# Token-shift layer: pair scores inside receptance and gate tiles, banks of both engines, the below-diagonal work shared anew

## What is computed

```python
def rwkv7_time_mix(h, mu, w_r, w_k, w_v, w_o, w0, w1, w2, a0, a1, a2, g1, g2, k_k, k_a, r_k, ln_g, ln_b):
    xx = jnp.pad(h, ((0, 0), (1, 0), (0, 0)))[:, :-1] - h
    xr, xw, xk, xv, xa, xg = [h + xx * mu[i] for i in range(6)]
    r = xr @ w_r
    w = -jax.nn.softplus(-(w0 + jnp.tanh(xw @ w1) @ w2)) - 0.5
    k = xk @ w_k
    v = xv @ w_v
    a = jax.nn.sigmoid(a0 + (xa @ a1) @ a2)
    g = jax.nn.sigmoid(xg @ g1) @ g2
    ...
    def step(state, inp):
        r_t, d_t, k_t, v_t, kk_t, a_t = inp
        sa = jnp.einsum('bhij,bhj->bhi', state, -kk_t)
        state = (state * d_t[:, :, None, :] + sa[..., None] * (kk_t * a_t)[:, :, None, :]
                 + v_t[..., None] * k_t[:, :, None, :])
        return state, jnp.einsum('bhij,bhj->bhi', state, r_t)
```

## Time and profile before

| what | us |
|---|---|
| median of three runs | 1712.45 |
| profiled execution, device time | 1714.71 |
| its span, first to last instruction | 1712.9 |
| PE busy (share of the span) | 1660.0 (97%) |
| DVE busy | 1031.1 (60%) |
| ACT busy | 397.2 (23%) |
| POOL busy | 274.6 (16%) |

### The profile page before, as it was taken

One profiled execution on the slowest core, in us unless ns is written; L12 is line 12 of the kernel. 1 busy time (PEld: TensorE's weight loads), 2 busy tenths in 40 slices (PEclk: granted clock), 3 DMA queues, 4 the chain that ended last, 5 costly groups with the idle time before them and its releaser, 6 DMA issues.

```text
span 1712.9 us, 26789 instructions
## 1 busy us (share of the span) xinstructions
PE 1660.0 (97%) x11020; PEld 1314.6 (77%) x11020; DVE 1031.1 (60%) x1990; ACT 397.2 (23%) x1033; POOL 274.6 (16%) x356
## 2 busy tenths in 40 slices
PE   8999999999999999999999899999999999998998
PEld 7997488776699946999467779699946777676774
DVE  5777344754287664876578766487673554625563
ACT  2010023532210102011036532311002233222331
POOL 3324000000023200323001323122200220012100
PEclk9999999998999999999999999999999999999999
DMA  8767654221445453645444320345456973469830
GB/s 267 224 190 228 145 132 147 74 74 52 145 153 192 149 196 124 196 149 195 149 117 148 122 98 2 98 148 184 161 181 118 167 109 94 99 93 182 118 104 24
DMA packets 197113, 237.68 MB, mean 139 GB/s; under 512 B 28349, under 2 KB 177265, under 8 KB 196737
## 3 DMA queue, kind: packets, MB, share of 16 engines
q1 hardware_dynamic: 192016, 225.36, 47.2%
q0 software_dynamic: 4960, 10.61, 2.2%
q10 hardware_dynamic: 16, 0.00, 0.0%
HBM read 232.69 MB, written 1.07 MB: 136 GB/s over the span
## 4 chain that ended last, share of the span: by engine, by line
PE 88%; DVE 5%; ACT 2%; DMA 2%; issue 1%; POOL 0%; SPq 0%; DVEq 0%; POOLq 0%; ACTq 0%
PE ps L605 29%; PE ps L277 23%; PE ps L671 14%; PE ps L522 6%; PE ps L615 3%; DMA arena<-arena 2%; PE ps L1939 2%; PE ps L2578 1%; PE ps L2590 1%; PE ps L1956 1%; PE ps L2609 1%; PE ps L335 1%; PE ps L2604 1%; PE ps L1719 1%; DMA ring<-in_ffn_w_gate 0%
## 5 line engine op out<-in xcount | busy, mean ns | idle before, releaser
L277 PE MATMUL ps<-hT,ring 128*128 128x272 f32 (+3 forms) x1664 | 353.2, 368 | 1.8 <-ACT hT L359 1.3
L277 PEld LDWEIGHTS ps<-hT,ring 128*128 128x128 f32 x1664 | 286.3, 193 | 51.1 <-issue 6.8
L605 PE MATMUL ps<-arena,ring 128*128 128x128 f32 x1280 | 162.5, 275 | 0.0
L671 PE MATMUL ps<-ring,arena 128*128 128x512 f32 x352 | 155.9, 593 | 1.7 <-DVE more L776 1.7
L866 POOL TENSOR_TENSOR arena<-arena 128x128 f32<-128x128 f32 x44 | 36.7, 834 | 740.3 <-DVE arena L790 396.6
L605 PEld LDWEIGHTS ps<-arena,ring 128*128 128x128 f32 x1280 | 152.6, 192 | 0.0
L605 PE MATMUL ps<-hT,ring 128*128 128x128 f32 x1280 | 150.1, 275 | 0.0
L605 PEld LDWEIGHTS ps<-hT,ring 128*128 128x128 f32 x1280 | 146.5, 192 | 0.0
L671 PEld LDWEIGHTS ps<-ring,arena 128*128 128x128 f32 x352 | 66.6, 190 | 87.2 <-issue 87.2
L605 PE MATMUL ps<-arena 128*128 128x128 f32 x960 | 120.3, 275 | 0.0
L605 PEld LDWEIGHTS ps<-arena 128*128 128x128 f32 x960 | 113.6, 192 | 0.0
(11 more groups left out here) (490 smaller groups left out, 2693.9 us busy)
## 6 DMA issues: line engine op xcount, KB each, us to landing
ring<-in_ffn_w_gate SPq DMA_DIRECT2D x44, 1024.0 KB, 5.4
ring<-in_ffn_w_up SPq DMA_DIRECT2D x44, 1024.0 KB, 7.2
ring<-in_ffn_w_down SPq DMA_DIRECT2D x44, 1024.0 KB, 5.0
ring<-in_w_in SPq DMA_DIRECT2D x32, 1024.0 KB, 14.2
ring<-in_ab_w_in SPq DMA_DIRECT2D x12, 1024.0 KB, 5.2
ring<-in_w_out SPq DMA_DIRECT2D x8, 1024.0 KB, 5.0
ring<-in_ab_w_out SPq DMA_DIRECT2D x6, 1024.0 KB, 4.8
ring<-in_c_w_k SPq DMA_DIRECT2D x4, 1024.0 KB, 6.3
```

Source lines behind the costliest of these rows:

```text
L277: last = nc.tensor.matmul(o, l, r, start=(i == 0), stop=(i == len(pairs) - 1))
L605: m = nc.tensor.matmul(o, left[:, k, :], right[:, k, :], start=(k == 0), stop=(k == 3))
L671: return nc.tensor.matmul(ps[:, BANK[i], :], hid[p][:, left, :], right, start=(p == 0), stop=(p == LAST))
```

## The change

The scores of pairs 0, 1 and 2 are now computed inside r4 (after 3 of its 8 products), r5 (after 7) and r7 (after 3), and those of pair 3 inside the gate's first layer. Each pair takes its first bank from ScalarE's ring and its second from VectorE's, before the tile around it takes its own. ScalarE still empties every bank below the diagonal (of VectorE's ring too, where it raises `dve_out`) and copies the diagonals of the first banks and of (0, 1). VectorE copies the diagonals of (1, 1), (2, 1) and (3, 1), and leaves L2281 and L2282 to ScalarE. The bonus product and the first gate pair go ahead of the 32-row rounds; the rounds of chunk 1 (`m32`, `t32` with t = 1) go to ScalarE's banks and copies.

```diff
             def r_product(j):
-                tile_product("r", j, S_R + j // 2, MB[3], (2 if j == 0 else 1) if j % 2 == 0 else 0)
+            def r_product(j, p2=None, at_c=0):
+                slot = S_R + j // 2
+                if j % 2 == 0:
+                    take_slot(pe, slot)
+                o = score_banks(p2) if p2 is not None else None
+                n = turn_a("r", j)
+                for c in range(KD):
+                    if o and c == at_c:
+                        pair_scores(p2, o)
+                    m = nc.tensor.matmul(bank_a(n)[:, 0:S], slot8(slot)[:, c, (j % 2) * P:(j % 2 + 1) * P], MB[3][:, c, :],
+                                         start=(c == 0), stop=(c == KD - 1))
...
-            pair_scores(0)
-            r_product(4)
-            pair_scores(1)
-            r_product(5)
-            pair_scores(2)
+            r_product(4, 0, 3)
+            r_product(5, 1, 7)
             r_product(6)
-            pair_scores(3)
-            r_product(7)
+            r_product(7, 2, 3)
...
+            last = score_banks(3)
             n = turn_a("g1")
             group(bank_a(n)[:, 0:S], [(g1[:, c, 0:P], MB[5][:, c, :]) for c in range(KD)], 1)
+            pair_scores(3, last)
...
+            def bank_32(t, name):
+                return bank_d(turn_d(name, t)) if t == 0 else bank_a(turn_a(name, t))
...
+            take_slot(pe, s)
+            pe.wait_ge(act_out, job["g1",])
+            bonus_product()
+            gate_pair(0)
+            pe.wait_ge(act_out, job["x", 3, 0])
+            pe.wait_ge(dve_out, job["x", 3, 1])
             pe.wait_ge(sc_dve, 1)
             m32_product(0)
-            take_slot(pe, s)
-            pe.wait_ge(act_out, job["g1",])
-            gate_first(0, 0)
             m32_product(1)
-            gate_first(0, 1)
-            gate_first(1, 0)
+            gate_pair(1)
             pe.wait_ge(sc_dve, 2)
             t32_product(0)
-            gate_first(1, 1)
-            bonus_product()
             pe.wait_ge(sc_act, 1)
             t32_product(1)
-            for r, (t, h) in enumerate((t, h) for t in range(T) for h in range(2)):
...
@@ rwkv_act
+            def below_out(p2, hh):
+                _, left, corner = score_parts(score_bank(p2, hh), p2, hh)
+                nc.scalar.activation(*left, ACT.Copy)
+                nc.scalar.activation(*corner, ACT.Copy).then_inc(dve_out if hh else act_out, 1)
+
             def scores_out(p2):
...
+                act_a()
+                diagonal_out(p2, 0)
+                below_out(p2, 0)
...
             key_root(7)
+            decays(6)
+            diagonal_out(0, 1)
+            decays(7)
             scores_out(1)
-            decays(6)
             r_out(5)
-            decays(7)
-            scores_out(2)
             r_out(6)
-            scores_out(3)
+            act_a()
+            diagonal_out(2, 0)
+            diagonal_out(3, 0).then_inc(x_out, 1)
+            below_out(2, 0)
             r_out(7)
+            act_a()
+            below_out(3, 0)
+            below_out(0, 1)
+            act.wait_ge(x_out, 2)
+            for p2 in (1, 2, 3):
+                below_out(p2, 1)
...
+            gate_out(0)
+            b = next_a().rearrange("p (h n) -> p h n", h=SH)
+            nc.scalar.activation(m32[32:64, SH:2 * SH, :], b[32:64], ACT.Copy)
+            nc.scalar.activation(m32[96:P, SH:2 * SH, :], b[96:P], ACT.Copy).then_inc(act_out, 1)
+            gate_out(1)
+            b = next_a().rearrange("p (h n) -> p h n", h=SH)
+            nc.scalar.activation(tts[1][0:32, :, 32:64], b[0:32], ACT.Copy)
+            nc.scalar.activation(t64[32:64, SH:2 * SH, 0:32], b[32:64], ACT.Copy)
+            nc.scalar.activation(tts[1][64:96, :, 96:P], b[64:96], ACT.Copy).then_inc(act_out, 1)
...
@@ rwkv_dve
-            diag, left, corner = score_parts(next_d(), 3, 1)
-            for o, b in diag:
-                m = nc.vector.tensor_copy(o, b)
+            dve_d()
+            for p2 in (1, 2, 3):
+                for o, b in score_parts(next_d(), p2, 1)[0]:
+                    m = nc.vector.tensor_copy(o, b)
             m.then_inc(x_out, 1)
...
-            nc.vector.tensor_copy(*left)
-            nc.vector.tensor_copy(*corner).then_inc(dve_out, 1)
```

More of the change, by code:

```diff
@@ L1708, in pair_scores @@
                             if t == 1 and i == 1:
-                                m.then_inc(to_dve if p2 == 3 and hh == 1 else to_act, 1)
+                                m.then_inc(to_dve if hh else to_act, 1)
             need_h(pe, pe_h.n)
@@ L1837, in t64_product @@
                                         start=True, stop=True, skip_group_check=True)
+            def bank_32(t, name):
+                return bank_d(turn_d(name, t)) if t == 0 else bank_a(turn_a(name, t))
             def m32_product(t):
-                n = turn_d("m32", t)
+                b = bank_32(t, "m32")
                 for h in range(SH):
@@ L1843, in m32_product @@
                     for g in range(2):
-                        m = nc.tensor.matmul(bank_d(n)[64 * g + 32:64 * g + 64, 32 * h:32 * h + 32],
+                        m = nc.tensor.matmul(b[64 * g + 32:64 * g + 64, 32 * h:32 * h + 32],
                                              at0[:, ch, :] if g == 0 else at64[64:96, ch, 32:64], t64[64 * g:64 * g + 32, ch, 0:32],
                                              start=True, stop=True, skip_group_check=True)
-                        if ch == 0 and g == 0:
-                            m.then_inc(slot_used, 1)
-                m.then_inc(to_dve, 1)
+                m.then_inc(to_act if t else to_dve, 1)
             def t32_product(t):
-                pe.wait_ge(dve_out, job["m32", t])
-                n = turn_d("t32", t)
+                pe.wait_ge(act_out if t else dve_out, job["m32", t])
+                b = bank_32(t, "t32")
                 for h in range(SH):
@@ L1857, in t32_product, with gate_pair @@
                         lo, hi = slice(64 * g, 64 * g + 32), slice(64 * g + 32, 64 * g + 64)
-                        nc.tensor.matmul(bank_d(n)[lo, 32 * h:32 * h + 32], m32[hi, ch, :], tts[t][hi, h, hi],
-                                         start=True, stop=True, skip_group_check=True)
[L1860 to L1866, removed]
+                        m = nc.tensor.matmul(b[lo, 32 * h:32 * h + 32], m32[hi, ch, :], tts[t][hi, h, hi],
+                                             start=True, stop=True, skip_group_check=True)
+                        if ch == 0 and g == 0:
+                            m.then_inc(slot_used, 1)
+                    m = nc.tensor.matmul(b[32:64, 32 * h:32 * h + 32], tts[t][32:64, h, 32:64], m32[32:64, ch, :],
+                                         start=True, stop=True, skip_group_check=True)
+                m.then_inc(to_act if t else to_dve, 1)
+            def gate_pair(t):
+                for h in range(2):
+                    m = nc.tensor.matmul(bank_a(turn_a("g2", t, h)), sg1[:, t * P:(t + 1) * P], slot2(s)[:, 0, h * 512:(h + 1) * 512],
+                                         start=True, stop=False)
+                    if t == 0 and h == 0:
+                        m.then_inc(slot_used, 1)
+                for h in range(2):
+                    r = 2 * t + h
+                    rows = slice(32 * r, 32 * r + 32)
+                    nc.tensor.matmul(bank_a(job["g2", t, h]), sg2[rows, :], slot2(s)[rows, 1, h * 512:(h + 1) * 512],
+                                     start=False, stop=True).then_inc(to_act, 1)
             def bonus_product():
@@ L2010, in next_a, with score_bank, diagonal_out @@
                 return bank_a(n)
-            def scores_out(p2):
-                for hh in range(1 if p2 == 3 else 2):
-                    diag, left, corner = score_parts(next_a(), p2, hh)
-                    for o, b in diag:
[L2016 to L2020, removed]
+            def score_bank(p2, hh):
+                n = job["x", p2, hh]
+                act.wait_ge(to_dve if hh else to_act, n)
+                return (bank_d if hh else bank_a)(n)
+            def diagonal_out(p2, hh):
+                for o, b in score_parts(score_bank(p2, hh), p2, hh)[0]:
+                    m = nc.scalar.activation(o, b, ACT.Copy)
+                return m
+            def below_out(p2, hh):
+                _, left, corner = score_parts(score_bank(p2, hh), p2, hh)
+                nc.scalar.activation(*left, ACT.Copy)
+                nc.scalar.activation(*corner, ACT.Copy).then_inc(dve_out if hh else act_out, 1)
+            def scores_out(p2):
+                act_a()
+                diagonal_out(p2, 0)
+                below_out(p2, 0)
             def key_root(j):
@@ L2110, in rwkv_act, with gate_out @@
                 m.then_inc(act_out, 1)
-            for t in range(T):
+            def gate_out(t):
                 for h in range(2):
```

42 lines of the change are left out of this document (17 added, 25 removed).

## The result

| | before | changed |
|---|---|---|
| median of 20 runs, us | 1713.93 | 1720.68 |
| lowest and highest, us | 1709.68, 1721.96 | 1713.28, 1726.1 |
| profiled execution and its span, us | 1714.7, 1712.9 | 1713.28, 1711.5 |

The account below looks back on a forecast made before the run. TensorE, with 88% of the chain, was taken as the bound. Value products 3.0 us ahead, -1.5 for the clock, +0.6 - 0.45 later gave 1.6 faster: 1710.9 us from 1712.45, range 1705.5 to 1715.5.

Parts of the forecast that it names:

- The failed step: From m64 on: nothing edited, weight loads' slot releases all come earlier or within 1 us, so no cost.
- the sum: Whole change: value products 3.0 ahead, clock's fall -1.5, later part +0.6 - 0.45, giving 1.6 us faster.
- the walk: Step-by-step timing of the engines through the token-shift stage; finds TensorE's wait moved to receptance tile 7, 4.1 us.
- The clock's fall: Behind the 4.1 us wait before receptance tile 7: granted clock falls to half, costing 1.5 us.
- rival D: VectorE's later solve ends last, delaying the first t32 or m32 round; 0.4 to about 2 us slower; chance 0.15.
- ScalarE's list: From 943.8, copies, roots and decays without gap sum to 10.7 us; pair 1's first bank comes free at 954.6.
- The value products: Behind the gate's first layer: first one starts at 966.2 against 969.1, 3.0 us ahead, 1.5 with the clock's fall.
- The solve: On VectorE: transpose at 965.6 against 962.99, then near 967, four later; t32 rounds keep 0.6 us of slack.
- The copies on ScalarE: Second 32-row rounds: 32x512 copy taken as 0.59 us against VectorE's 0.68; TensorE waits 0.3 to 0.5 us at m64.
- The wait on L2113: Between gate seconds and token rows: TensorE's 0.6 us wait for this gate copy goes.
- Within 0.5%: Whole kernel's time: chance 0.92 of staying within about 0.5% (8.6 us), 0.05 for faster, 0.03 for slower.
- The range: Whole kernel's time: 1705.5 to 1715.5 us, around a forecast of 1710.9.

Follow-up runs that it names:

- Run 1: Changed kernel with the gate weights' slot release put back to the first token transpose; median 1718.71 us, ratio to before 1.0014.
- run 5: Changed kernel with late slot release, pair 1's first bank emptied early, and gate pair 1 split ahead of and between t32 rounds; median 1711.78 us, ratio 0.9992.
- run 6: Each half of the change alone: new scores with the tail of before, ratio 1.0118; scores of before with the new tail, ratio 1.0052.
- run 2: Changed kernel with ScalarE emptying pair 1's first bank right after key root 7; median 1712.45 us, ratio to before 0.9980.
- run 7: New scores with the tail of before, plus ScalarE emptying pair 1's first bank right after key root 7; median 1711.29 us, ratio to before 0.9980.
- run 4: Kernel before with an extra 1 MB copy within HBM, started by the first t32 product; ratio to before 1.0012.
- run 3: Changed kernel with both the slot release put back and pair 1's first bank emptied early; median 1711.40 us, ratio to before 0.9987.
- the front alone: Kernel before with only the new scores, banks and shared diagonals, tail from the first 32-row round unchanged; median 1738.62 us, ratio 1.0118.

## Why the prediction was wrong

- **The failed step** is one clause of the sum: "From m64 on nothing is edited, and the weight loads wait for slots six loads ahead whose releases all come earlier or within 1 us." I used it to price the moved release at nothing. As a fact it holds: the gate slot's release comes 2.9 us earlier from r3's end (68.0 for 70.9). What fails is that an earlier load costs nothing. What matters is not when the load can start, but what TensorE is doing while it runs. The load lands on a dense train of small instructions and on the fetch of those behind it, and TensorE stands 2.4 to 3.3 us in the next group. Run 1 shows the release alone (2.76 to 1.12), run 5 the train (1.35 to none). Price of the step, by the chunk product's start from r3's end: 5.9 later where the forecast had it 1.6 earlier.
- **What the change does to TensorE's order** I costed only through its waits. Gate and bonus products moved from between the t32 rounds and behind them to places ahead of them, and I counted their time; that they had also parted the trains of small products was not in the walk.
- **The clock's fall** was in the sum once, behind r7, and near its price (1.8 measured, 1.5 forecast). A second one, at the stop, lengthened the busy time by 3.9 us and was in no case. In rival D I had the size of such a thing ("a clock fall of twice the length"), with the wrong cause.
- **ScalarE's list was right**: 10.7 us from 943.8 forecast, 10.9 measured from the start of S0's first bank (940.86) to the end of L2045; r7 waits 3.80 for 4.1. On ScalarE:

```profile
946.79 1.56 ACT L2039 ACTIVATE arena<-ps 32x128 f32<-32x128 f32 x4
...
949.71 1.55 ACT L2039 ACTIVATE arena<-ps 32x128 f32<-32x128 f32 x4
951.27 0.38 ACT L2044 ACTIVATE hT<-ps 128x256 f32<-128x256 f32 x1
951.55 0.25 ACT L2045 ACTIVATE more<-ps 32x128 f32<-32x128 f32 x1
```

- **The value products**, 1.4 ahead forecast with the clock's fall, 0.6 measured: r7 starts 0.2 later from r3's end than in the walk (17.5 for 17.3), the half clock took 0.3 more, and the first value product waits 0.56 for 0.3.
- **The solve** starts 4.9 us later from r3's end than before (30.5 for the earlier trace rows's 25.6), forecast 4. In the changed kernel nobody waits for it: VectorE is ready at 1000.8 for the t32 rounds, TensorE comes at 1002.4. Rival D did not happen. In the order of run 6, with nothing ahead of the rounds, the same late solve costs 2.20 us.
- **The copies on ScalarE**: 32 x 512 took 0.59 us against VectorE's 0.68, as taken from the 128 x 512 copy.

```profile
1004.72 0.59 ACT L2167 ACTIVATE arena<-ps 32x512 f32<-32x512 f32 x1 [1.09 <-PE ps L1876]
```

- **The wait on L2113** (0.6) did go, and m64 did not wait for these copies. That is the stop's doing: in run 5, which has none, m64 waits 0.71 us for them, where the forecast had 0.3 to 0.5.
- **Slips in the walk**: the list of the idling before leaves out 0.36 us before the third score group, r6 is 8.0 us ahead by the walk's own figures and not 7.7, and the value products 2.9 and not 3.0. Only the last is in the sum.
- **The chances.** "Within 0.5%" held. The range did not: it was made of waits on semaphores alone, and its upper end had no case in which a stop of no known releaser and a ten-microsecond clock fall come together.

## What to carry to other kernels

A slot release is the start time of a transfer. When an edit moves one, look at what the engines run in the 3 to 5 us after it, and keep the load off dense trains of small matmuls; put a few long products between such trains instead of ahead of them. Where two engines share the emptying of banks, walk the list of the slower one in its written order and put the bank that TensorE needs first at its head: that one reordering (run 2) turned 0.34% slower into 0.2% faster, with the interval below 1, and run 7 reached the same. These two are the versions to take; run 5 has the shortest stretch, but its median does not show it.

## What the runs showed of the hardware that I had not expected

**TensorE can run out of instructions.** The stops of 1.1 to 3.3 us have no releaser, full DMA engines lengthen them, and spacing the train removes the one of 1.35. This is the reading that fits all eight profiles with the new tail, seven with a stop and the spaced one without. The packets of q8 in the kept traces bear it out: at each of these seven stops, and at that of run 4, TensorE goes on 1.3 to 1.6 us behind a packet's end, though the stops range from 0.89 to 3.31 us. With no load under way (runs 1 and 3) that packet starts 1.5 to 1.6 us behind the first t32 product; with the load that this product releases, 2.8 to 3.5. The Trainium skill, "Runtime: NRT & Kernel Launch", section "Instruction fetch mechanics", says that the sequencer fetches the next page by a DMA queue of its own while it runs the current one, and that the cost is mostly hidden. Here it was not: 384 matmul and weight-load records in 2.2 us were followed by a stop in all profiles that had them undivided.

**The clock can keep its low level long.** Behind the stop of 3.80 us it was at 0.50 for 3.4 us, at those of 2.40 to 3.31 in the token rows for 7 to 10 us, though TensorE was busy without a break behind them; behind 1.35 (run 3) it still fell, for 3.4 us, behind 1.12 (run 1) it did not, and behind the 0.89 of run 4 it fell for 7. So the length of the stop alone does not order these. In the front alone it was at 0.50 for 51 us (1022 to 1073) in a stage that runs at 0.99 to 1.00 in the kernel before, and full clock lay between (1005 to 1022) and the last long stop, the 2.20 us one at 997. What decides between the two levels there stays open, and nothing was tried on it.
